# The last two down-projection units of each feed-forward, taken token tile by token tile, in a two-block transformer kernel on one core

## The reference

```python
D_MODEL, SEQ, D_FF = 1024, 512, 2816

def rms_norm_2(x, g):
    y = xf * lax.rsqrt(jnp.mean(xf * xf, axis=-1, keepdims=True) + EPS)
    return (y * g.astype(jnp.float32)).astype(x.dtype)

def swiglu(h, w_gu, w_down):
    gate, up = jnp.split(h @ w_gu, 2, axis=-1)
    return (jax.nn.silu(gate) * up) @ w_down

# second_block
f = swiglu(rms_norm_2(h, ffn1_pre_g), ffn1_w_gu, ffn1_w_down)
h = h + 0.5 * rms_norm_2(f, ffn1_post_g)
z = rms_norm_2(h, mix_pre_g) @ w_in
...                       # two attentions, output projection, post norm, residual
f = swiglu(rms_norm_2(h, ffn2_pre_g), ffn2_w_gu, ffn2_w_down)
h = h + 0.5 * rms_norm_2(f, ffn2_post_g)      # the output
```

## Time and profile before

| what | us |
|---|---|
| three runs | 1937.8, 1940.85, 1941.66 |
| median | 1940.85 |
| profiled execution, first to last instruction | 1939.3 |
| PE busy in it | 1823.9 (94%) |
| DVE busy | 970.1 (50%) |
| ACT busy | 863.5 (45%) |
| POOL busy | 254.5 (13%) |

### The profile page before, as it was taken

The page is one execution under the profiler, slowest core; times in us unless marked ns, Lnnn a source line. Parts: engine busy times, 40 slices in busy tenths (PEclk is TensorE's granted clock), DMA queues, the critical chain, the costliest instruction groups (busy, mean ns, idle before and its releaser), DMA issues.

```text
span 1939.3 us, 22676 instructions
## 1 busy us (share of the span) xinstructions
PE 1823.9 (94%) x8553; PEld 1431.7 (74%) x8553; DVE 970.1 (50%) x1549; ACT 863.5 (45%) x1355; POOL 254.5 (13%) x313
## 2 busy tenths in 40 slices
PE   8997999999779999979999999998788999999997
PEld 6885666667668888858888888786554878888886
DVE  4446344445469999964332342625555354423434
ACT  4235665552348888853223231424566143223222
POOL 4000532220001111200000000511223000000000
PEclk9997999999989999999999999998799999999999
DMA  7224011115469999672323332333000133224331
GB/s 208 87 69 130 23 43 46 44 44 190 180 240 373 389 384 382 242 231 66 109 90 94 100 96 98 88 106 98 12 22 23 47 86 96 92 92 109 87 108 54
DMA packets 161283, 246.31 MB, mean 127 GB/s; under 512 B 11586, under 2 KB 117281, under 8 KB 148256
## 3 DMA queue, kind: packets, MB, share of 16 engines
q1 hardware_dynamic: 152880, 232.30, 35.5%
q0 software_dynamic: 8304, 12.69, 2.2%
HBM read 239.15 MB, written 12.61 MB: 130 GB/s over the span
## 4 chain that ended last, share of the span: by engine, by line
PE 86%; DVE 5%; ACT 4%; issue 3%; POOL 1%; DMA 1%; DVEq 0%; SPq 0%; ACTq 0%; POOLq 0%
PE psum L434 25%; PE psum L436 24%; PE psum L435 24%; PE psum L599 3%; PE psum L579 3%; PE psum L568 2%; ACT warea_r L419 1%; PE psum L1269 1%; DVE xarea L1910 1%; POOL arena L699 1%; PE psum L1443 1%; DVE xarea L2280 1%; PE psum L1164 1%; PE psum L1096 0%; DMA arena<-y_assigned 0%
## 5 line engine op out<-in xcount | busy, mean ns | idle before, releaser
L425 DVE TENSOR_TENSOR warea_r<-warea,warea_r 128x2048 fp32r<-128x2048 f32 x110 | 255.3, 2322 | 331.6 <-ACT warea_r L419 331.4
L434 PE MATMUL psum<-tarea_r,warea_r 128*128 128x512 f32 x896 | 357.2, 399 | 3.8 <-DVE tarea_r L1920 3.8
L436 PE MATMUL psum<-tarea_r,warea_r 128*128 128x512 f32 x896 | 351.0, 392 | 0.0
L435 PE MATMUL psum<-tarea_r,warea_r 128*128 128x512 f32 x896 | 350.9, 392 | 0.0
L419 ACT ACTIVATE warea_r<-warea 128x2048 fp32r<-128x2048 f32 x110 | 209.7, 1907 | 271.0 <-PE psum L436 266.1
L434 PE MATMUL psum<-warea_r,arena_r 128*128 128x512 f32 (+1 forms) x768 | 300.4, 391 | 14.0 <-DVE warea_r L425 5.0
L436 PE MATMUL psum<-warea_r,arena_r 128*128 128x512 f32 (+1 forms) x768 | 297.5, 387 | 0.0
L435 PE MATMUL psum<-warea_r,arena_r 128*128 128x512 f32 (+1 forms) x768 | 297.2, 387 | 0.0
L434 PEld LDWEIGHTS psum<-tarea_r,warea_r 128*128 128x128 f32 x896 | 169.2, 189 | 45.0 <-issue 8.4
L436 PEld LDWEIGHTS psum<-tarea_r,warea_r 128*128 128x128 f32 x896 | 169.3, 189 | 36.3
L435 PEld LDWEIGHTS psum<-tarea_r,warea_r 128*128 128x128 f32 x896 | 169.4, 189 | 33.8 <-issue 0.7
(11 more groups left out here) (325 smaller groups left out, 2482.6 us busy)
## 6 DMA issues: line engine op xcount, KB each, us to landing
warea<-in_ffn_w_gu SPq DMA_DIRECT2D x88, 512.0 KB, 5.0
warea<-in_w_in SPq DMA_DIRECT2D x40, 512.0 KB, 4.6
warea<-in_ffn_w_down SPq DMA_DIRECT2D x40, 512.0 KB, 4.4
arena<-in_w_up SPq DMA_DIRECT2D x16, 1024.0 KB, 8.1
tarea<-in_w_up SPq DMA_DIRECT2D x16, 1024.0 KB, 7.2
tarea<-in_w_down SPq DMA_DIRECT2D x16, 1024.0 KB, 7.5
warea<-in_w_gate SPq DMA_DIRECT2D x14, 1024.0 KB, 7.7
harea<-in_w_gate SPq DMA_DIRECT2D x14, 1024.0 KB, 7.9
```

Source lines behind the costliest of these rows:

```text
L425: dve.tensor_tensor(w_lo[:, u % 2, :], raw_of(u), w_hi[:, u % 2, :].bitcast(f32), ALU.subtract)\
L434: nc.tensor.matmul(out, high, by_high, start=first, stop=False)
L435: nc.tensor.matmul(out, high, by_low, start=False, stop=False)
L436: return nc.tensor.matmul(out, low, by_high, start=False, stop=last)
```

## The change

- TensorE: the loop over down units stops after j = 6 in the odd halves. `down_by_tile` then takes j = 8 and j = 10 together: banks 0 to 5 get their three chunks one bank after another, each with its `fd_psum`; banks 6 and 7 get two chunks, `unit_done` is raised, and then they get the last chunk. It begins with a wait for `split_lo` of the second of the two units. The matmuls are as many as before. The five filler products after tail 1 are gone.
- DVE: `tail` takes banks as they come, and between them makes each tile's variance, reciprocal and residual sum. For tile 3 the sum of squares comes in two halves that are added in the variance; its gain multiplication is DVE's. At the end of tail 2 the last residual sum is made in two halves.
- POOL multiplies the gain on tiles 0, 1 and 2 (`tail_gains`).
- ACT: `tail_squares` squares a tile and takes its root one after the other, tile 3 in two halves. The split of unit `AT_MID`, which stood before the squares of tail 1, now stands behind them. The squares are written to other bytes of the arena (`TAIL`).
- SP: the last tile of the output is sent as two transfers of 128 x 512.

```diff
@@ sync
-            for t in range(NT):
+            for t in range(NT - 1):
                 sp.wait_ge(s["res_ready"], 4 * 4 + t + 1)
                 sp.dma_start(out[0, t * P:(t + 1) * P, :], xres[:, t, :]).then_inc(s["out_dma"], 16)
-            sp.wait_ge(s["out_dma"], 16 * NT)
+            for h in range(2):
+                sp.wait_ge(s["res_ready"], 4 * 4 + NT + h)
+                sp.dma_start(out[0, (NT - 1) * P:NT * P, 512 * h:512 * h + 512], xres[:, NT - 1, 512 * h:512 * h + 512])\
+                    .then_inc(s["out_dma"], 16)
+            sp.wait_ge(s["out_dma"], 16 * (NT + 1))
@@ gpsimd
+            def tail_gains(n):
+
+                pool.wait_ge(s["gain_in"], 16 * (n + 1))
+                for t in range(NT - 1):
+                    pool.wait_ge(s["sumsq"], 4 * (1 + 2 * n) + n // 2 + t + 1)
+                    nc.gpsimd.tensor_tensor(hn[:, t, :], hn[:, t, :], gain, ALU.mult).then_inc(s["premul_pool"], 1)
...
-            premultiplied(1)
+            tail_gains(1)
@@ tensor
-                for j in range(0, HALF, 2):
+                for j in range(0, HALF - 3 if g % 2 else HALF, 2):
...
+                if g % 2:
+                    down_by_tile(u0 + UNITS - 2)
+
+            def down_by_tile(u):
+
+                pe.wait_ge(s["split_lo"], u + 2)
+
+                def share(m, c):
+                    t, hf = divmod(m, 2)
+                    v, n, j = (u, 2, HALF - 3) if c < HALF - 1 else (u + 1, 1, HALF - 1)
+                    return products(ps[m], hid_hi[:, c, P * t:P * t + P], hid_lo[:, c, P * t:P * t + P],
+                                    *weights(v, 512 * (n * hf + c - j), 512), False, c == HALF - 1)
+
+                for m in range(6):
+                    for c in range(HALF - 3, HALF):
+                        mm = share(m, c)
+                    mm.then_inc(s["fd_psum"], 1)
+                for m in (6, 7):
+                    for c in (HALF - 3, HALF - 2):
+                        mm = share(m, c)
+                mm.then_inc(s["unit_done"], 1)
+                for m in (6, 7):
+                    share(m, HALF - 1).then_inc(s["fd_psum"], 1)
...
-            keep_busy(ps[7], 5)
             raw_features(3, lambda t: pe.wait_ge(s["res_ready"], 8 + t + 1))
@@ scalar
+            def tail_squares(evacuated):
...
+                warm()
+                for t in range(NT - 1):
+                    act.wait_ge(s["f_evac"], evacuated + 2 * t + 2)
+                    square(t, 0, D, ss[:, t:t + 1]).then_inc(s["sumsq"], 1)
+                    root(rstd[:, t:t + 1])
+                act.wait_ge(s["f_evac"], evacuated + 7)
+                square(NT - 1, 0, 512, ss[:, 31:32]).then_inc(s["sumsq"], 1)
+                act.wait_ge(s["f_evac"], evacuated + 8)
+                square(NT - 1, 512, D, ss[:, NT - 1:NT]).then_inc(s["sumsq"], 1)
+                root(rstd[:, NT - 1:NT])
...
-                if g < 3:
+                if g % 2 == 0:
                     split_high(u0 + UNITS)
...
-            post_squares(lambda t: 8 + 2 * t + 2)
+            tail_squares(8)
+            split_high(AT_MID)
             split_high(AT_MID + 1)
             late_features(3)
@@ vector, in tail(g)
+                def finish(t):
+                    inverse_root(rstd[:, t:t + 1])
+                    dve.wait_ge(s["premul_pool"], 4 * (n - 1) + t + 1)
+                    add_rows(t, 0, D).then_inc(s["res_ready"], 1)
...
+                evacuate(0)
+                evacuate(1)
+                evacuate(2)
+                row_variance(0)
+                evacuate(3)
+                finish(0)
...
+                evacuate(6)
+                row_variance(2)
+                evacuate(7)
+                finish(2)
+                dve.wait_ge(s["sumsq"], before + NT)
+                chained(V.tensor_scalar(ss[:, 30:31], ss[:, 31:32], f2 / D, f2 * 1e-6, ALU.mult, ALU.add))
+                row_variance(NT - 1)
+                chained(V.tensor_tensor(hn[:, NT - 1, :], hn[:, NT - 1, :], gain, ALU.mult))
+                inverse_root(rstd[:, NT - 1:NT])
+                for a, b in ((0, D),) if g == 1 else ((0, 512), (512, D)):
+                    add_rows(NT - 1, a, b).then_inc(s["res_ready"], 1)
```

More of the change, by code:

```diff
@@ L219, in build_blocks @@
     LO_AT, HI_AT, AR = RAW_AT + 4096, RAW_AT + 8192, 17808
+    TAIL = AR - 4096 - 336
     areas = []
@@ L1021, in _ @@
             load_gain(3)
-            premultiplied(3)
+            tail_gains(3)
         @block.tensor
@@ L1583, in post_squares, with square @@
                 root(rstd[:, 0:NT])
+            def tail_squares(evacuated):
+                def square(t, a, b, dst):
+                    return nc.scalar.activation(arena[:, TAIL + t * D + a:TAIL + t * D + b], hn[:, t, a:b], ACT.Square, accum_out=dst)
+                warm()
[8 more added lines that the diff above has]
+                root(rstd[:, NT - 1:NT])
             split_high(0)
@@ L1833, in _ @@
             ffn_half(3)
-            post_squares(lambda t: 32 + 2 * t + 2)
+            tail_squares(32)
         @block.vector
         def _(dve):
-            steps_done, roots, gains_used, norms = counter(), counter(), counter(), counter()
+            steps_done, roots, gains_used, norms, tails = counter(), counter(), counter(), counter(), counter()
             V = nc.vector
@@ L1853, in inverse_root, with summed @@
                 chained(V.reciprocal(ap, ap))
+            def summed():
+                return 4 * norms[0] + tails[0]
             def row_rstd():
                 norms[0] += 1
-                dve.wait_ge(s["sumsq"], 4 * norms[0])
+                dve.wait_ge(s["sumsq"], summed())
                 variance(rstd[:, 0:NT], ss[:, 0:NT], D).then_inc(s["var_ready"], 1)
@@ L1892, in premultiply @@
                 dve.wait_ge(s["gain_in"], 16 * (gains_used[0] + 1))
-                dve.wait_ge(s["sumsq"], 4 * norms[0] + t + 1)
+                dve.wait_ge(s["sumsq"], summed() + t + 1)
                 V.tensor_tensor(hn[:, t, :], hn[:, t, :], gain, ALU.mult).then_inc(s["premul"], 1)
@@ L1901, in post_norm @@
                         premultiply(t)
-                dve.wait_ge(s["sumsq"], 4 * norms[0] + 4)
+                dve.wait_ge(s["sumsq"], summed() + 4)
                 f2 = factor ** -2
@@ L1912, in post_norm, with tail, evacuate, row_variance @@
                 norms[0] += 1
+                gains_used[0] += 1
+                V.memset(nmax[:, 0:1], 0.0).then_inc(s["gain_used"], 1)
+            def tail(g):
+                n, f2, before = tails[0] + 1, 4.0, summed()
+                def evacuate(m):
+                    t, hf = divmod(m, 2)
+                    part = hn[:, t, 512 * hf:512 * hf + 512]
+                    dve.wait_ge(s["fd_psum"], 8 * g + m + 1)
+                    V.scalar_tensor_tensor(out=part, in0=ps[m], scalar=late[(2, 4)[g // 2]][:, t:t + 1], in1=part,
+                                           op0=ALU.mult, op1=ALU.add).then_inc(s["f_evac"], 1)
+                def row_variance(t):
+                    dve.wait_ge(s["sumsq"], before + (t + 1 if t < NT - 1 else NT + 1))
+                    if t < NT - 1:
+                        ins = V.tensor_scalar(rstd[:, t:t + 1], ss[:, t:t + 1], f2 / D, f2 * 1e-6, ALU.mult, ALU.add)
+                    else:
+                        ins = V.scalar_tensor_tensor(out=rstd[:, t:t + 1], in0=ss[:, t:t + 1], scalar=f2 / D, in1=ss[:, 30:31],
+                                                     op0=ALU.mult, op1=ALU.add)
+                    ins.then_inc(s["var_ready"], 1)
+                def add_rows(t, a, b):
+                    return V.scalar_tensor_tensor(out=xres[:, t, a:b], in0=hn[:, t, a:b], scalar=rstd[:, t:t + 1],
+                                                  in1=xres[:, t, a:b], op0=ALU.mult, op1=ALU.add)
+                def finish(t):
+                    inverse_root(rstd[:, t:t + 1])
+                    dve.wait_ge(s["premul_pool"], 4 * (n - 1) + t + 1)
+                    add_rows(t, 0, D).then_inc(s["res_ready"], 1)
+                dve.wait_ge(s["gain_in"], 16 * (gains_used[0] + 1))
+                evacuate(0)
[4 more added lines that the diff above has]
+                finish(0)
+                evacuate(4)
+                row_variance(1)
+                evacuate(5)
+                finish(1)
+                evacuate(6)
[9 more added lines that the diff above has]
+                    add_rows(NT - 1, a, b).then_inc(s["res_ready"], 1)
+                norms[0] += 1
+                tails[0] += 1
@@ L2316, in ffn_half @@
                 else:
-                    for m in range(8):
-                        t, hf = divmod(m, 2)
-                        part = hn[:, t, 512 * hf:512 * hf + 512]
-                        dve.wait_ge(s["fd_psum"], 8 * g + m + 1)
-                        V.scalar_tensor_tensor(out=part, in0=ps[m], scalar=late[(2, 4)[g // 2]][:, t:t + 1], in1=part,
-                                               op0=ALU.mult, op1=ALU.add).then_inc(s["f_evac"], 1)
```

(2 more changed lines are left out.)

6 lines of the change are left out of this document (2 added, 4 removed).

## The result

| | before | after |
|---|---|---|
| median, us (19 runs each) | 1938.65 | 1947.48 |
| lowest to highest | 1932.24 to 1944.62 | 1940.82 to 1954.32 |
| ratio, with 95% interval | | 1.0042 (1.0032 to 1.0053) |
| profiled execution, first to last instruction | 1939.3 | 1950.4 |

The changed kernel is slower by 8.1 us (6.2 to 10.3). The forecast was 1948.2, in a range of 1943.5 to 1951, and 7.4 us slower.

What follows compares the result with a forecast made beforehand. Bound: 25.7 us without PE's matmuls in two tails. Tail 1 (4.7 - 1.7 + 2.0 + 0.3 = +5.3) and tail 2 (4.7 - 4.6 + 2.0 = +2.1) add 7.4 to 1940.85: 1948.2 us, range 1943.5 to 1951.

Steps and rivals of the forecast that it cites:

- The hold: Start of both tails: PE waits for unit j = 10's split before the last 72 matmuls; 4.7 us each tail.
- The clock: First of the 72 matmuls: PE's 4.4 us idle time drops the clock to 1.2 GHz; 2.0 us each tail.
- the clock stays up: Rival, both tails: the clock does not fall during the holds; 1944.0 us, no measurable change; chance 0.14.
- Tail 1 behind the hold: From the 72 matmuls' start to the next products: 27.9 us against 29.6, 1.7 saved, bounds 1.0 and 2.5.
- ScalarE's two splits: Behind tail 1's last root: two ACT splits of 1.90 us each now precede the squares and high parts.
- Tail 2 behind the hold: From the 72 matmuls' start to the end: 24.5 us against 29.1, 4.6 saved, bounds 3.9 and 5.0.
- the last transfer is then half as large: End of tail 2: the smaller output transfer saves 0.65 us, so last sum to end takes 2.7 instead of 3.3.
- the forecast's own lower bound of 3.9: Tail 2: the saving if the smaller last transfer lands no sooner; 3.9 us.
- The clock at the next products: Products behind tail 1: lower clock after a 5 us PE pause costs 0.3 us more, between -1.7 and 0.9.
- 0.6 us of cover: Both tails: POOL's gain multiplications end before DVE wants them, 0.6 us to spare; price 0.
- the rival on POOL: Rival, both tails: POOL's multiplications run late and tile 2's sum waits; up to +3.6 us, 1951.8; chance 0.09.
- the rival of the forecast: Both tails: the clock stays up if a 4.4 us PE pause is still short enough; 1944.0 us; chance 0.14.

Runs made afterwards that it cites:

- e1: Kernel before, with only the wait for the low part of unit j = 10 moved ahead of unit j = 8's first matmul; ratio to before 1.0082.
- e7: Changed kernel, with the last down unit of the odd halves split over its 1024 used columns only; ratio to before 1.0018.
- e2: Changed kernel without the hold: j = 8's two chunks go to banks 0 to 3 before the wait for the last split; ratio to before 1.0007.
- e8: Changed kernel with e7's half splits, e4's order, e5's one transfer, and j = 8's products for banks 0 and 1 before the wait; ratio to before 0.9934.
- e4: Changed kernel, ScalarE splitting AT_MID between tile 2's square and root, and AT_MID + 1 after the features' high parts; ratio to before 1.0038.
- e5: Changed kernel, with the last output tile summed in one step and sent in one transfer; ratio to before 1.0046.
- e3: Changed kernel with six filler products adding zeros to bank 7 ahead of the hold in each odd half; ratio to before 1.0028.
- e9: e2, with POOL waiting for tile 0's residual sum before multiplying tile 1; one run, 1947.43 us against 1938.78 of the kernel before.

## Why the forecast was right, step by step

The forecast of +7.4 us stands against 8.1 (6.2 to 10.3). Part of why the time of 1948.2 came so near 1947.48 is luck: it was added to a median of three runs, 1940.85, where 19 runs give 1938.65.

- **The hold**: forecast 4.7 in each tail, measured 4.39 of idle time, and a start 4.28 behind the start of ACT's split instead of 0.26 ahead of it, so 4.5 late; PE is released by DVE's part of the split, as the forecast had it from the earlier trace rows. e1 shows that it is not hidden, e7 that it scales with the split, e2 and e8 that it goes when PE has j = 8 to work on.
- **The clock**: forecast 2.0 in each tail; the last bank came 1.7 and 2.6 late, 4.3 together. Over e1, e4 and e5 it is 1.6 to 3.0 for the same pause. e3, which keeps PE busy in it, pays 0.15: the rival "the clock stays up" is priced about rightly and did not happen. (Of the pauses it went by, one was read a little short: 0.87 over 517 to 518 puts the rise at 517.26, so 3.2 us at the lower level and not 3.0.)
- **Tail 1 behind the hold**: forecast 1.7 saved. The products lie 29.19 behind the start of the 72 matmuls; without the 1.7 of the clock that is 27.5, and before it was 29.6: 2.1 saved. That ScalarE's two splits would be late next was right, e4 shows it.
- **Tail 2 behind the hold**: forecast 4.6 saved, and here one term was mis-sized. The last sum was to come at 21.8; it came at 24.32, of which 2.61 is the clock: 21.7. The step that failed is "the last transfer is then half as large, 0.65 us less: 2.7". It landed 2.1 after its issue, which is the 0.65 less, but the end came 1.8 after the landing where the earlier trace rows have 0.5, and the term of 2.7 measured 3.95. So 3.4 was saved in tail 2, under the forecast's own lower bound of 3.9. The bound assumed that a transfer which lands no sooner is the worst case; what lies behind the landing was in no bound.
- **The clock at the next products**: forecast +0.3. It was low from the first product at 1250.15 until almost 1255.0, 4.8 us, where the mean of the earlier trace rows amounts to 3.4; at 0.47 lost of each, that is some 0.7 more. The trace has it directly: ACT's third split behind the first product of both kernels starts 35.53 us after that product before and 36.17 after, 0.64 more. PE's pause was as forecast, 4.75 against 5. PE in the changed kernel, last microsecond at the lower level:

```profile
1254.00:1255.00 1.00, 1.00 (x4) 0.52 0.16 48
```

- **POOL**: 0.6 us of cover was taken as enough, and it was. Its instructions in tail 2:

```profile
1931.07 2.39 POOL L915 TENSOR_TENSOR harea<-harea,garea 128x1024 f32<-128x1024 f32 x1 [358.44 <-ACT arena L1622]
1935.08 2.40 POOL L915 TENSOR_TENSOR harea<-harea,garea 128x1024 f32<-128x1024 f32 x1 [1.62 <-ACT arena L1622]
1939.17 2.40 POOL L915 TENSOR_TENSOR harea<-harea,garea 128x1024 f32<-128x1024 f32 x1 [1.68 <-ACT arena L1622]
```

They stand 1.6 and 1.7 apart, so no sum met two of them in a row. The rival was real all the same: e2 and e9 ran into it, with last sums at 24.3 to 24.8 where e8 has 21.7.

By the intervals from the split: products 33.5 against 29.3 (+4.2), end 32.6 against 28.8 (+3.7), clock at the products +0.6: 8.5 us. That is the measured loss within its interval, and the working above gives the same parts. (The 0.6 lies inside the stretch of 667.7 us that is equally long in both profiles; the rest of that stretch was 0.6 shorter after, which is well within what it varies by.) The near hit of 7.4 is in part misses that cancel: the saving of tail 2 was put 1.2 too high, against 0.4 too low for tail 1, 0.3 too high for the two holds, and 0.3 too low for each of the two clock terms. The stated range ended at 1951, though its own terms reached 1951.4 and the rival on POOL 1951.8; the result did not come near. What no single kernel measured is how this loss divides in the medians; e1, e2 and e8 alone have intervals clear of the changed kernel's; the medians of e3, e4, e5 and e7 can't be told from it.

## What to carry to other kernels

A wait that is merged from the middle of a loop to its front exposes whatever used to run under the first part; with a double buffer, the buffer's last reader sets how early the preparation can start, so idle engines ahead of it prove nothing. Do first what needs only the unit that is ready, just enough to cover the wait (a burst of results can crowd the engines behind), and prepare only the columns that are used. Size the pause with the clock that falls in it, and compare stretches with a common event as zero, not whole spans, when the change is a few us of 1940.

## What the runs showed of the hardware that was not expected

- A DVE sum with SBUF operands takes 1.28 us alone and 3.33 to 3.42 when POOL begins a second 2.4 us multiplication just as the sum is released by the first (e2, e9). Moving POOL by one tile moves the stall by one tile.
- A PE pause of 2.46 us was followed by the lower clock in one tail of e7 and one of 2.47 in the other was not; nor was one of 2.65 in the kernel before. In that kernel the clock also fell at 1244.3, 1.5 us into products that followed a pause of only 1.87 us and the turning of the tiles. So the length of one pause does not decide it, and the rival of the forecast, which went by length alone, stood on less than it seemed. PE before, behind tail 1:

```profile
1243.00:1244.00 1.00, 1.00 (x5) 1.00 0.85 122
1244.00:1245.00 1.00, 1.00 (x4) 0.65 0.90 335
1245.00:1246.00 1.00, 1.00 (x4) 0.50 1.07 369
```

- From the last landing to the last instruction it takes 0.3 to 2.3 us, and neither the number of transfers nor their spacing explains which.
- The same code reaches the same point, the split of j = 10 in tail 1, anywhere from 1206.08 to 1219.66 us; the 668 us of unchanged work between the two tails vary by 4.5.
